# Top-k and the next query cut into four parts among the expert dots and the V sets, and the next layer's first modulation sums moved ahead

## The reference

```
mod = silu(c) @ ada_w[l] + ada_b[l];  sh1, sc1, g1, sh2, sc2, g2 = split(mod, 6)
x  = x + g1 * (mixer(modulate(rms_norm(x), sh1, sc1) @ w_in[l]) @ w_out[l])
xf = modulate(rms_norm(x), sh2, sc2)
q  = xf @ w_query[l]                        # 8 heads of 2 x 256
s  = q . sub_keys[l];  vals, idx = top_k(s, 16)      # both halves, 128 keys each
cand = vals0[:, None] + vals1[None, :];  top_s, pos = top_k(cand, 16)
eidx = idx0 * 128 + idx1 at pos;  g = softmax(top_s)
h  = xf . expert_u[eidx];  act = gelu(h) * g
x  = x + g2 * sum_k act_k * expert_v[eidx_k]
```

## Time and profile before

| | us |
|---|---|
| median of 3 runs (lowest, highest) | 3718.97 (3710.23, 3719.86) |
| the profiled execution's own time | 3713.7 |
| its span, first to last instruction | 3711.8 |
| layer 0: front; expert stage | 0 to 344; 344 to 1117 |
| layer 1: front; expert stage | 1117 to 1456; 1456 to 2226 |
| second stack | 2226 to 3712 |

### The profile page before, as it was taken

One profiled execution on the slowest core, in us unless ns is written; L12 is line 12 of the kernel. 1 busy time (PEld: TensorE's weight loads), 2 busy tenths in 40 slices (PEclk: granted clock), 3 DMA queues, 4 the chain that ended last, 5 costly groups with the idle time before them and its releaser, 6 DMA issues.

```text
span 3711.8 us, 34410 instructions
## 1 busy us (share of the span) xinstructions
PE 2547.4 (69%) x12111; PEld 1746.3 (47%) x12111; DVE 2080.9 (56%) x4572; ACT 827.9 (22%) x1271; POOL 1119.8 (30%) x1028
## 2 busy tenths in 40 slices
PE   5986444444345986444444337799889979989898
PEld 2454222222002444222222005589778967977697
DVE  4544666667634545666666634655445554555554
ACT  0110100000000110100000004344434433444343
POOL 0001777677760001777777750000000000000000
PEclk9998776677556998776677568699969976998699
DMA  7723999999987713999999985145414531544153
GB/s 287 281 72 113 371 386 373 384 374 379 367 330 254 281 71 118 374 382 372 384 379 372 383 314 189 38 162 195 148 38 159 191 115 46 181 172 146 46 181 125
DMA packets 306600, 884.64 MB, mean 238 GB/s; under 512 B 21192, under 2 KB 31520, under 8 KB 306336
## 3 DMA queue, kind: packets, MB, share of 16 engines
q0 software_dynamic: 147456, 536.94, 37.9%
q1 hardware_dynamic: 159008, 346.05, 26.0%
HBM read 881.86 MB, written 1.05 MB: 238 GB/s over the span
## 4 chain that ended last, share of the span: by engine, by line
PE 48%; POOL 19%; DVE 13%; issue 13%; DMA 4%; ACT 2%; SPq 1%; DVEq 0%; POOLq 0%; ACTq 0%
POOL proj L1805 9%; PE lin L576 8%; PE lin L829 6%; PE lin L830 6%; PE lin L831 6%; POOL ring L1818 5%; POOL vbuf L1818 4%; PE psS L613 3%; DMA proj<-in_expert_u,eidx 2%; DVE proj L1575 2%; PE lin L642 2%; PE psT L556 2%; PE psT L829 2%; PE psT L830 2%; PE psT L831 2%
## 5 line engine op out<-in xcount | busy, mean ns | idle before, releaser
L1575 DVE CUSTOM_DVE_ANT_0 proj<-proj,tokb 128x1024 f32<-128x1024 f32 x512 | 611.1, 1224 | 410.9 <-DMA proj<-in_expert_u,eidx 384.7
L1805 POOL DMA_INDIRECT proj<-in_expert_u,eidx x512 | 545.1, 1065 | 927.3 <-DVEq L1553 704.9
L1282 DVE TENSOR_TENSOR weights_split<-ring,weights_split 128x1024 fp32r<-128x1024 f32 (+1 forms) x376 | 451.8, 1208 | 515.4 <-ACT weights_split L1093 514.9
L784 PE MATMUL lin<-ring,rowb 128*32 128x512 f32 x896 | 225.9, 1032 | 523.7 <-DMA ring<-in_expert_v,pT 302.8
L1093 ACT ACTIVATE weights_split<-ring 128x1024 fp32r<-128x1024 f32 (+1 forms) x376 | 391.7, 1046 | 570.3 <-PE lin L831 357.5
L784 PE MATMUL lin<-vbuf,rowb 128*32 128x512 f32 x1024 | 186.1, 871 | 260.4 <-DMA vbuf<-in_expert_v,pT 153.4
L784 PEld LDWEIGHTS lin<-ring,rowb 128*32 128x32 f32 x896 | 37.1, 157 | 669.2 <-DMA ring<-in_expert_v,pT 312.6
L576 PE MATMUL lin<-ring,xT 128*128 128x512 f32 x768 | 342.4, 607 | 5.6 <-DVE xT L1234 3.4
L1818 POOL DMA_INDIRECT vbuf<-in_expert_v,pT x256 | 293.1, 1145 | 78.1 <-issue 77.8
L1818 POOL DMA_INDIRECT ring<-in_expert_v,pT x224 | 249.3, 1113 | 68.3 <-issue 67.7
L576 PEld LDWEIGHTS lin<-ring,xT 128*128 128x128 f32 x768 | 148.8, 195 | 192.4 <-issue 184.7
(11 more groups left out here) (236 smaller groups left out, 4590.8 us busy)
## 6 DMA issues: line engine op xcount, KB each, us to landing
ring<-in_mlp_w_up SPq DMA_DIRECT2D x32, 2048.0 KB, 8.1
ring<-in_mlp_w_down SPq DMA_DIRECT2D x32, 2048.0 KB, 7.6
ring<-in_ada_w SPq DMA_DIRECT2D x24, 2048.0 KB, 13.1
ring<-in_w_in SPq DMA_DIRECT2D x16, 2048.0 KB, 12.0
ring<-in_w_query SPq DMA_DIRECT2D x16, 2048.0 KB, 13.1
ring<-in_diff_w_in SPq DMA_DIRECT2D x12, 2048.0 KB, 8.0
ring<-in_moba_w_in SPq DMA_DIRECT2D x6, 2048.0 KB, 8.2
ring<-in_w_attn_o SPq DMA_DIRECT2D x4, 2048.0 KB, 11.7
```

Of the source, the lines that this page charges most:

```text
L784: mm = pe.matmul(lin[32 * b:32 * b + 32, 2 * half + t, :], wst[:, cb % 2, 4 * b + s, :], vrow(SETROWS * s + b)[:, half * 512:(half + 1) * ...
L1282: dve.tensor_tensor(part(p, 1, kind, w), raw_piece(slot, p, kind, w), part(p, 0, kind, w).bitcast(F32), ALU.subtract).then_inc(lo_ready, 1)
L1575: dve.tensor_tensor_reduce(ubuf[:, n % GB, :], ubuf[:, n % GB, :], tokb[:, t, :], 1.0, 0.0, ALU.mult, ALU.add, hdot[:, cb, k:k + 1]).then_ ...
L1805: pool.indirect_dma_start(out=ubuf[:, (16 * cb + k) % GB, :], out_offset=None, in_=table["u"], in_offset=bass.IndirectOffsetOnAxis(ap=eidx ...
```

## The change

**In the expert stage.** `topk` is cut into `topk_part` 0 to 3. Parts 0 to 2 run between groups of four dots of the chunk two ahead of which they rank, and part 3 after the weights. `query` is cut into `query_keys`, four `query_rows` (one after each V set of a head's first chunk) and `key_scores`. ACT's order is changed with it.

**At the front.** The first four modulation units leave `FIRST_UNITS`. Their sums for layer 0 are made before the layer loop. Those of the other layer are made in each layer during the output linears, from loads into parts of `proj` and `vbuf` that are free then. The wide parameters move behind two ring units and get a semaphore of their own.

```
-FIRST_UNITS = ([("ada", n) for n in range(4)]
-               + [("in", 0), ("ada", 4), ("in", 1), ("ada", 5), ("in", 2), ("ada", 6), ("in", 3), ("in", 4),
+FIRST_UNITS = ([("in", 0), ("ada", 4), ("in", 1), ("ada", 5), ("in", 2), ("ada", 6), ("in", 3), ("in", 4),
...
 SP
-            sp.dma_start(const[:, :], T["consts"][:, 0:CRES]).then_inc(s_const, 16)
-            sp.dma_start(x[:, :, :], T["x"][0].rearrange("(t p) d -> p t d", p=P)).then_inc(s_const, 16)
+            sp.dma_start(cact[:, :], T["c"].rearrange("a (k p) -> p (a k)", p=P)).then_inc(s_c, 16)
+            for n in range(NMIX):
+                if n == 2:
+                    sp.dma_start(x[:, :, :], T["x"][0].rearrange("(t p) d -> p t d", p=P)).then_inc(s_const, 16)
+                sp.dma_start(ring[:, n, :, :], cols_of(T["ada_w"][0], n * UC, UC)).then_inc(pre_ld[n], 16)
+            sp.dma_start(const[:, :], T["consts"][:, 0:CRES]).then_inc(s_const, 16)
...
+                sp.wait_ge(s_ada, 8)
+                for n in range(NMIX):
+                    if n >= 2:
+                        sp.wait_ge(acc_ready, 8 + n - 1)
+                    for t in range(2):
+                        sp.dma_start(mix_at[n % 2][t], cols_of(T["ada_w"][1 - l], n * UC, UC)[:, 4 * t:4 * t + 4, :]).then_inc(mix_ld[n % 2], 16)
+                    if n >= 2:
+                        query_load(n - 2, n - 2, True)
...
 PE
+            def mix_sum(n, ready, done):
+                acc = ada_acc[:, n % 2, :]
+                pe.wait_ge(*ready)
+                for j in range(4):
+                    mm = pe.matmul(psS[:, 0, 256 + 4 * n + j:256 + 4 * n + j + 1], acc[:, j * P:(j + 1) * P],
+                                   cst("iota")[:, 1:2], start=True, stop=True, skip_group_check=True)
+                mm.then_inc(done, 1)
...
             pe.wait_ge(s_const, 32)
+            for n in range(NMIX):
+                mix_sum(n, (pre_acc, n + 1), pre_sum)
...
-                pe.wait_ge(s_par, 160)
+                pe.wait_ge(s_par, 80)
...
+                        if asked:
+                            query_rows(h + 2, j, s)
...
                         weights_by_pair(2 * hp + j, j, 0)
-                        expert_sum(2 * hp + j, j, 0)
+                        query_keys(2 * hp + 2 + j, j)
+                        expert_sum(2 * hp + j, j, 0, asked=True)
+                        key_scores(2 * hp + 2 + j)
                         weights_by_pair(2 * hp + j, j, 1)
-                        query(2 * hp + 2 + j, j, False)
                         expert_sum(2 * hp + j, j, 1)
...
 ACT
                 query_copies(0)
+                query_copies(1)
                 with act.Fori(0, PH // 2 - 1) as hp:
-                    query_copies(2 * hp + 1)
-                    for t in range(NT):
-                        expert_weights(2 * hp, 0, t)
-                    query_copies(2 * hp + 2)
-                    for t in range(NT):
-                        expert_weights(2 * hp + 1, 1, t)
-                query_copies(PH - 1)
+                    for j in range(2):
+                        expert_weights(2 * hp + j, j, 0)
+                        query_copies(2 * hp + 2 + j)
+                        expert_weights(2 * hp + j, j, 1)
...
 DVE
+            dve.wait_ge(s_cact, 1)
+            for n in range(NMIX):
+                dve.wait_ge(pre_ld[n], 16)
+                if n >= 2:
+                    dve.wait_ge(pre_sum, n - 1)
+                partial_sums(ada_acc[:, n % 2, :], [ring[:, n, k, :] for k in range(KC)], pre_acc)
...
                 for n in range(4):
+                    if n < 2:
+                        next_mix_unit(n)
                     dve.wait_ge(lin_done, C.lin + 1)
...
                         dve.tensor_tensor_reduce(ubuf[:, n % GB, :], ubuf[:, n % GB, :], tokb[:, t, :], 1.0, 0.0,
                                                  ALU.mult, ALU.add, hdot[:, cb, k:k + 1]).then_inc(h_ready, 1)
+                        if ranked and k % 4 == 3 and k < 12:
+                            topk_part(h + 1, 1 - j, t, k // 4)
...
+                    if ranked:
+                        topk_part(h + 1, 1 - j, t, 3)
...
                             dots(2 * hp + j, j, t)
-                            topk(2 * hp + j + 1, 1 - j, t)
                             stationaries(2 * hp + j, j, t)
```

More of the change, by code:

```diff
@@ L323, in program @@
         s_const = sem("const_loaded")
+        s_c = sem("c_loaded")
+        s_wide = sem("wide_params_loaded")
+        pre_ld = [sem(f"first_mix_unit_loaded{i}") for i in range(NMIX)]
+        pre_acc = sem("first_mix_partial_sums_ready")
+        pre_sum = sem("first_mix_sums_done")
+        mix_ld = [sem(f"next_mix_slot_loaded{i}") for i in range(2)]
         s_par = sem("params_loaded")
@@ L433, in unit @@
                     sp.wait_ge(*used[n - RING])
+                else:
+                    sp.wait_ge(pre_acc, n + 1)
                 used.append(used_up)
@@ L693, in _ @@
                 pe.wait_ge(pl_cp, 1)
+                pe.wait_ge(s_wide, 80)
                 for g in range(NPG):
@@ L719, in _ @@
                     linear(C, xT, KC, ring[:, slot, :, :], UC)
+                for n in range(2, NMIX):
+                    mix_sum(n, (acc_ready, 9 + n), s_ada)
                 norm(C)
@@ L725, in _, with query_keys @@
                 qbase = C.slot[0]
-                def query(h, j, first):
+                def query_keys(h, j):
                     wait_loop(pe, sk_ld[j], 16 if isinstance(h, int) and h < 2 else (h - j) * 8 + 16)
@@ L754, in query @@
                     mm.then_inc(ps_done, 1)
+                def query(h, j):
+                    query_keys(h, j)
+                    for part in range(4):
+                        query_rows(h, j, part)
+                    key_scores(h)
                 def indices_by_pair(c, cb):
@@ L1395, in head_rms, with partial_sums @@
                 dve.wait_ge(hn_rs, ready)
+            def partial_sums(acc, w, ready):
+                link(dve.tensor_scalar(acc, w[0], cact[:, 0:1], None, ALU.mult))
+                for k in range(1, KC):
+                    ins = dve.scalar_tensor_tensor(out=acc, in0=w[k], scalar=cact[:, k:k + 1], in1=acc,
+                                                   op0=ALU.mult, op1=ALU.add)
+                    if k < KC - 1:
+                        link(ins)
+                ins.then_inc(ready, 1)
             def ada_unit(n):
@@ L1436, in _ @@
                 dve.wait_ge(p_col, 1)
-                dve.wait_ge(s_cact, 1)
-                for n in range(4):
-                    ada_unit(n)
                 mod_columns(0, 48)
@@ L1515, in topk, with topk_part @@
                 def topk(h, j, t):
+                    for part in range(4):
+                        topk_part(h, j, t, part)
+                def topk_part(h, j, t, part):
                     cb = NT * j + t
                     restart_chain()
-                    if t == 0:
+                    if t == 0 and part == 0:
                         wait_loop(dve, ps_done, h + 1)
@@ L1521, in topk @@
                         dve.sem_inc(ps_used, 1)
-                    for q in range(2):
+                    if part < 2:
+                        q = part
                         top16(topb[:, 2 * t + q, 0, :], topb[:, 2 * t + q, 1, :], NKEY, vals[:, q, :], idxu[:, q, :])
-                    link(dve.tensor_copy(idxf[:, :, :], idxu[:, :, :]))
+                        return
                     grid = [P, TOPK, TOPK]
@@ L1566, in take_indices, with dots @@
                     dve.tensor_copy(eidxT[:, cb % 4, :], idx_at(cb)).then_inc(it_used, 1)
-                def dots(h, j, t, ahead=True):
+                def dots(h, j, t, ahead=True, ranked=True):
                     cb = NT * j + t
```

118 lines of the change are left out of this document (68 added, 50 removed).

## The result

The changed kernel takes 3745.6 us, median of five runs (3737.7 to 3750.0), against 3716.9 us for the kernel before in the same comparison: the ratio is 1.0076, 95% interval 1.0056 to 1.0097. It is slower by 0.8%. The profiled execution has a span of 3735.7 us, 23.9 us over that of before.

A forecast was written before the change was run, and what follows sets the result against it. POOL's own stream of gathers was taken to set the expert stage's pace. The terms summed as 3713.7 + 90 (stages) - 38.5 + 4 (fronts) + 2 (output linears) = 3771, stated as 3772 us, range 3715 to 3825.

The forecast's parts named there:

- POOL paces the stage: Mid expert stage: 389 gathers at 1.24 us, 0.32 us a dot of excess and 20 us of waits make 563 us.
- The chain of 29.4 us, 34.7 at back edges: Once a head, from last V row through V set 3, query, Exp, Gelu to POOL's next gather; +28.5 us, chunk 0 to 10.
- Behind chunk 10, +6 us: Rest of a layer's expert stage: the chain once more, 32 groups and 58 dots, 206.7 us against 200.5.
- The start, +10 us: Expert stage's start: part 0 waits for head 1's scores, delaying the fourth U group; +10 us a layer, bounds 5 and 15.
- The query in pieces costs PE nothing else: Expert stage on PE: scores, query pieces and their loads add no further cost beyond the chain and the start.
- Front of layer 1, -38.5 us: SP's first row to first linear, 53.1 us before, shortens by 38.5 us, bounds -34 and -40.
- Front of layer 0, +4, and output linears, +2 us: Layer 0's first linear comes at 61 us instead of 56.83; extra sums at both layers' output linears add 2 us.
- ACT's order costs nothing: Rival, expert stage: V set 3 lands early or POOL has slack, so only waits go; 3650 us, chance 0.14 with the other fast rival.
- The spreading pays: Rival, expert stage: spread dots cost 0.04 us each, 3650 us; break-even 0.18; chance 0.14 with the other fast rival.
- The slow clock: Rival, PE: query parts run at the low clock throughout, landing takes 9 us; 3840 us, chance 0.13 with the failing front.
- The halves: Rival: chain and start cost 50 us, the front gives 32, so they cancel within 0.3% of 3719; chance 0.07.
- the front's part: Rival: it fails, constants or c holding up layer 0 more than layer 1 gains; 3810 us, chance 0.13 with the slow clock.

The follow-up runs named there:

- half_dots: `act_fixed` with dots over 512 of the 1024 columns, the other half of each dot product left out: 3609.9 us, ratio 0.9712.
- start_fixed: `act_fixed` with head 1's query on PE moved right behind the token transposes at the expert stage's start: 3624.5 us, ratio 0.9754.
- act_fixed: The changed kernel with ACT's query copy behind Exp and Gelu of a head's second chunk, PE's scores behind that chunk's weights product: 3646.9 us, ratio 0.9797.
- early_last_part: The changed kernel with PE making the last query part behind V set 2 and not V set 3, ACT's order as changed: 3660.1 us, ratio 0.9833.
- query_parts_only: The changed kernel with top-k whole again at the chunk's end, query and ACT's order as changed: 3830.0 us, ratio 1.0289.
- start_early: `start_fixed` with the last query part behind V set 2: 3848.7 us on a chip where the kernel before took 3908.5, ratio 0.9872.
- half_rows: `half_dots` with U gathers that fetch only 2 KB a row, from a table of half rows: 3557.1 us, ratio 0.9555.
- front_only: The kernel before with only the front part of the change: 3684.5 us, ratio 0.990.

## Why the prediction was right, and where its size was off

The forecast was 3772 us, slower; measured were 3745.6, slower, inside the range. The loss itself is 28.7 us by the medians, where the forecast had 53 over its median. It is the difference of two larger terms of opposite sign, and each was off by 11 to 21 us to the same side, so the net size holds less well than the way it went. By its steps:

- **POOL paces the stage, 1.24 us a gather plus excess plus waits.** Shown: the account closes before and after, and in `half_dots` the gathers alone stay at 0.94 us. The "0.32 us a dot" is the dots' doing, but it is no constant. It depends on how the dots lie: 0.32 before, 0.22 to 0.26 with the change, 0.175 in `start_fixed`.
- **The chain of 29.4 us, 34.7 at back edges; waits of 9 to 14 us, once a head.** Shown by both cures (`act_fixed`, `early_last_part`) and by the worsening (`query_parts_only`). The six waits were 8.1, 14.7, 8.6, 12.2, 6.7 and 8.6 us. DVE's wait, 16 us for Gelu in the forecast, was one for Exp, of 14.2 us in the mean. The chain's mean was 28.0 and 33.3 us, 1.4 us under the sum. Landing is not the reason: it took 5.6 us in the mean of the twelve heads and 5.7 were said. The V set is the larger part. It stands in the sum with 3.6 us and took 2.9 in the mean, since in four of the twelve heads it took 1.86 us, at a granted clock of 1.00 (2.4 GHz) and not 0.50 (1.2 GHz). The last query part with its handshake took 4.0 us, where 4.75 were said. Five heads at 1.4 us are 7 us, and chunk 0 to 10 came out 5.7 and 8.1 us under my 28.5: measured +22.8 and +20.4. These are the windows of V set 3 on PE in the fourth head and in the second:

```profile
740.69:742.55 1.86, 1.86 (x17) 0.42 (x17) 0.00 (x0) 0.00 (x0) 1.55 (x2) 1.00 1.02 410
539.25:542.83 3.58, 3.58 (x17) 0.60 (x17) 0.00 (x0) 0.00 (x0) 2.81 (x3) 0.50 0.99 398
```

- **Behind chunk 10, +6 us.** This step failed; it was -1.4 and -0.1. I took the excess at 0.32 us for 58 dots, 18.6 us. POOL needed 170 us there for 128 gathers, so excess and waits together were 11 us.
- **The start, +10 us.** The wait of the fourth group was as predicted, at 384.2 us, 42.8 us behind the first gather. The cost was 13 us. `start_fixed` got 8 to 11 us a layer back.
- **The query in pieces costs PE nothing else.** DVE waits 18.4 us in six times for PE's product of the weights, a wait that was not there before. With the chain cured it is 44.9 us, and the kernel is faster. No wait of POOL's shows it, so "nothing" held for POOL's waits; what the wait does to the spacing of the dots was not measured apart, since `start_early` gives no answer.
- **Front of layer 1, -38.5 us.** Measured -40.5: the first linear stands 12.7 us behind SP's first row and not 14.6.
- **Front of layer 0, +4, and output linears, +2 us.** The first linear came at 58.6 us, so +1.8; the constants had landed when PE's first sum began at 33.64 us (35 said), and c cost next to nothing, as DVE's first unit began at 9.85 us. But the first U gather stood 2.3 us earlier than before. Across the kernels with this front it lies between 341.0 and 346.5 us, so this term is lost in their spread.
- **The terms together.** Predicted were +90 for the stages and -32.5 for the fronts; measured in the profile are +68.8 and -43.3, with -1.6 behind. Two thirds of the miss are the stages (tail and chain, less the start), a third the fronts. The mechanism was right and both sizes leaned the same way.
- **The rivals.** "ACT's order costs nothing" is refuted: repaired, with its pair of lines on PE, it gives back some 100 us. "The spreading pays" was right as a mechanism and wrong for this kernel: the excess fell from 0.32 to 0.22 to 0.26 us a dot in the changed kernel, not to 0.04, and stayed above the break-even of 0.18. The slow clock did not come: the granted clock in the window was 0.70 against 0.66, and the last query part took 4.7 us in the chain shown. The halves didn't cancel (+68.8 and -43.3 us), and the front's part brought more than forecast.
- **The rule on the shared port pair** (the Trainium skill, SBUF — State Buffer, "SBUF: two separate sides") says that GpSimd is shut out while VectorE holds the ports. `half_dots` agrees: with dots of 0.69 us and not 1.22, the excess falls from 0.21 to 0.06 us a dot, and in `half_rows` to 0.10. I had drawn from it that spreading doesn't help since the dots stay as many. That was wrong here: the same number of full dots costs 0.33 us each in `front_only` and 0.21 in `act_fixed`. What in the schedule does it was not tried further.

## What to carry to other kernels

When a step is cut up and laid between others, look at the in-order engines that only pass its results on. Here one copy on ACT, the engine with the least to do, tied a chunk's weights to a transfer that had not landed. Moving either the copy or its input on PE removed the loss. Put what is asked for soonest first in such a queue, and let the part that waits for a late input stand last. And before taking work out of the end of a chunk, look whether it was filling a wait.

## What the runs showed of the hardware that I had not expected

A gather beside full dots took up to 1.99 us, and one without dots 0.94 us; how much of it is paid goes by the schedule (0.175 to 0.33 us a dot for the same 128x1024 dots, and 0.06 to 0.10 for half of the width), so a contention cost read from one schedule is not a constant for the next. The gathers' stream comes near 400 GB/s (404 in `half_dots`), with the DMA share at 1.02, and on one chip, where the kernel before was 5% slower, `start_early` got 336 GB/s in the window.
